# RWKV outputs of odd chunks with their two heads exchanged in PSUM

## The reference

```
def step(S, inp):
    r_t, w_t, k_t, v_t, kk_t, a_t = inp
    sa = jnp.einsum('bhvk,bhk->bhv', S, -kk_t)
    S = S * w_t[:, :, None, :] + sa[..., None] * (kk_t * a_t)[:, :, None, :] + v_t[..., None] * k_t[:, :, None, :]
    return S, jnp.einsum('bhvk,bhk->bhv', S, r_t)
...
y = _group_norm(y, ln_w, ln_b, RW_GN_EPS) + jnp.sum(r * k * r_k, -1, keepdims=True) * v
```

## Time and profile before

| what | us |
|---|---|
| median of 3 runs | 2271.08 (2270.03 to 2274.18) |
| profiled execution, its own time | 2267.93 |
| span in that execution | 2266.1 |
| PE busy | 2227.2 (98%) |
| POOL busy | 1742.7 (77%) |
| DVE busy | 1094.6 (48%) |
| ACT busy | 668.5 (30%) |

### The profile page before, as it was taken

One profiled execution on the slowest core, in us unless ns is written; L12 is line 12 of the kernel. 1 busy time (PEld: TensorE's weight loads), 2 busy tenths in 40 slices (PEclk: granted clock), 3 DMA queues, 4 the chain that ended last, 5 costly groups with the idle time before them and its releaser, 6 DMA issues. The chain is left out here.

```text
span 2266.1 us, 35428 instructions
## 1 busy us (share of the span) xinstructions
PE 2227.2 (98%) x14528; PEld 1715.4 (76%) x14528; DVE 1094.6 (48%) x1427; ACT 668.5 (30%) x1217; POOL 1742.7 (77%) x1228
## 2 busy tenths in 40 slices
PE   7999999999999999999999999999999999999999
PEld 5767777777778778777777677777777777777777
DVE  5023327566573762455260223386665647525542
ACT  5222322222221322443342222223233213324421
POOL 3677679688688999888637776896796799898884
PEclk9999999999999999999999999999999999999999
DMA  4623344333334545732436233443333354466223
GB/s 163 188 77 95 94 139 119 97 116 100 93 108 140 163 149 175 256 94 79 144 98 183 83 102 94 140 117 96 98 117 95 90 172 149 134 206 228 91 83 127
DMA packets 165475, 288.44 MB, mean 127 GB/s; under 512 B 28792, under 2 KB 36344, under 8 KB 163776
## 3 DMA queue, kind: packets, MB, share of 16 engines
q1 hardware_dynamic: 125216, 211.60, 31.4%
q10 hardware_dynamic: 40096, 74.57, 10.0%
HBM read 234.43 MB, written 51.68 MB: 126 GB/s over the span
## 5 line engine op out<-in xcount | busy, mean ns | idle before, releaser
L753 POOL TENSOR_SCALAR w_hi<-raw 128x512 fp32r<-128x512 f32 x552 | 902.3, 1635 | 322.5 <-PE ps_proj L794 275.9
L763 POOL TENSOR_TENSOR w_lo<-raw,w_hi 128x512 fp32r<-128x512 f32 (+1 forms) x640 | 846.0, 1322 | 153.7 <-ACT w_hi L1230 98.3
L794 PE MATMUL ps_proj<-h_hi,w_hi 128*128 128x512 f32 (+1 forms) x1760 | 725.2, 412 | 7.1 <-POOL w_lo L763 3.9
L794 PE MATMUL ps_proj<-h_lo,w_hi 128*128 128x512 f32 (+1 forms) x1760 | 688.9, 391 | 0.0
L794 PE MATMUL ps_proj<-h_hi,w_lo 128*128 128x512 f32 x1728 | 676.2, 391 | 0.0
L794 PEld LDWEIGHTS ps_proj<-h_hi,w_hi 128*128 128x128 f32 (+1 forms) x1760 | 330.2, 188 | 106.1 <-issue 27.3
L794 PEld LDWEIGHTS ps_proj<-h_lo,w_hi 128*128 128x128 f32 (+1 forms) x1760 | 329.6, 187 | 72.8
L794 PEld LDWEIGHTS ps_proj<-h_hi,w_lo 128*128 128x128 f32 x1728 | 326.1, 189 | 66.0 <-issue 7.7
L809 PE MATMUL ps_proj<-w_hi,h_hi 128*128 128x512 f32 x448 | 181.4, 405 | 0.4 <-POOL w_lo L763 0.4
L809 PE MATMUL ps_proj<-w_lo,h_hi 128*128 128x512 f32 x448 | 174.9, 390 | 0.0
L809 PE MATMUL ps_proj<-w_hi,h_lo 128*128 128x512 f32 x448 | 174.9, 390 | 0.0
(11 more groups left out here) (342 smaller groups left out, 2887.5 us busy)
## 6 DMA issues: line engine op xcount, KB each, us to landing
raw<-in_w_in_dram SPq DMA_DIRECT2D x480, 256.0 KB, 2.7
raw<-in_w_out_dram SPq DMA_DIRECT2D x128, 256.0 KB, 3.0
projected<-stage SPq DMA_DIRECT2D x116, 256.0 KB, 2.7
arena<-projected ACTq DMA_DIRECT2D x90, 256.0 KB, 3.1
out_dram<-arena ACTq DMA_DIRECT2D x7, 1024.0 KB, 4.8
gated_hi<-arena ACTq DMA_DIRECT2D x24, 256.0 KB, 2.6
gated_lo<-arena ACTq DMA_DIRECT2D x24, 256.0 KB, 3.2
h_hi<-gated_hi SPq DMA_DIRECT2D x8, 768.0 KB, 6.0
```

The lines of the kernel that those rows point to most:

```text
L753: nc.gpsimd.tensor_scalar(hi, src, 1.0, None, ALU.mult).then_inc(s_hi_split, 1)
L763: nc.gpsimd.tensor_tensor(lo, src, hi.bitcast(F32), ALU.subtract).then_inc(s_raw_split, 1)
L794: last = mm(ps_proj[rows, m, :], lhsT, rhs, start=(k == 0 and j == 0), stop=(k == KT - 1 and j == len(products) - 1))
```

## The change

The outputs of odd chunks are written with the two heads exchanged: head 0 to the upper partitions, head 1 to the lower. For the chunk's own outputs this changes the target partitions of the products alone. The carried products of odd chunks move from the diagonal quarters to the other two. ACT and DVE, which read these outputs, put the halves back: the one instruction over all chunks becomes three, one over even chunks with 128 partitions and two over odd chunks with 64 partitions each, reading one half and writing the other. In the table a tile moves from after line 1110 to before it, for every pair.

```
-    rw_carried=(3, 3, 3, 3), rw_gate=(13, 14, 13, 12),
+    rw_carried=(4, 4, 4, 4), rw_gate=(12, 13, 12, 11),
...
-                                mm(ps[half, 2 + c, fed], rw_vT[q, i, half], rw_gk[q, 4 * h + i, 64:P],
+                                mm(ps[halves[h ^ c], 2 + c, fed], rw_vT[q, i, half], rw_gk[q, 4 * h + i, 64:P],
                                    start=(i == 0), stop=False)
...
-                                mm(ps[half, 2 + c, fed], rw_pu[q, 4 * h + i, 64:P], rw_gb[q, 4 * h + i, 64:P],
+                                mm(ps[halves[h ^ c], 2 + c, fed], rw_pu[q, 4 * h + i, 64:P], rw_gb[q, 4 * h + i, 64:P],
                                    start=False, stop=False)
...
-                                last = mm(ps[half, 2 + c % 2, fed], rw_st[half, c, :],
+                                last = mm(ps[halves[h ^ (c % 2)], 2 + c % 2, fed], rw_st[half, c, :],
                                           rw_ar[half, c // 2, 1, 64 * (c % 2):64 * (c % 2) + 64],
...
-                        nc.scalar.activation(rw_kk.rearrange("p (i c t) -> p c i t", i=NT, c=2), y_parts, ACT.Square).then_inc(s_rw_y_squared, 1)
+                        squares = rw_kk.rearrange("p (i c t) -> p c i t", i=NT, c=2)
+                        nc.scalar.activation(squares[0:64, 1], y_parts[64:P, 1], ACT.Square)
+                        nc.scalar.activation(squares[64:P, 1], y_parts[0:64, 1], ACT.Square)
+                        nc.scalar.activation(squares[:, 0], y_parts[:, 0], ACT.Square).then_inc(s_rw_y_squared, 1)
...
-                        link(v.tensor_tensor(rw_yl.rearrange(in_parts, i=NT, c=2), rw_nr.rearrange(in_parts, i=NT, c=2), y_parts, MUL))
+                        scaled, scales = rw_yl.rearrange(in_parts, i=NT, c=2), rw_nr.rearrange(in_parts, i=NT, c=2)
+                        link(v.tensor_tensor(scaled[:, 0], scales[:, 0], y_parts[:, 0], MUL))
+                        link(v.tensor_tensor(scaled[0:64, 1], scales[0:64, 1], y_parts[64:P, 1], MUL))
+                        link(v.tensor_tensor(scaled[64:P, 1], scales[64:P, 1], y_parts[0:64, 1], MUL))
```

## The result

| what | before | after |
|---|---|---|
| median of 20 runs each, us | 2270.64 (2265.38 to 2274.18) | 2274.59 (2269.7 to 2277.23) |
| ratio, with its 95% interval | | 1.0014 (1.0008 to 1.0021) |
| profiled execution, us | 2267.93 | 2275.65 |

The ratio is +3.2 us at 2270.6 (1.8 to 4.8). The forecast was -0.8, and 2274.59 lies above the range, whose end was 2273.8. The prediction had put the smallest change that can be told from none at 0.2%; with 20 runs on each side the interval is narrower than that and lies wholly above 1. So this is a small loss, under the 0.2%, shown by many runs and by no single one.

A forecast was written before the change was run, and what follows sets the result against it. PE was taken as the bound, busy 2227.2 of 2266.1 us. Saving 2.8 us at line 1104 less 2.0 us of waits for DVE gave -0.8 us, 2270.3 us against the median 2271.08; range 2267.0 to 2273.8.

The forecast's parts named there:

- PE's part: Line 1104's carried products take 0.62 instead of 0.97 us, saving 0.35 a pair, 2.8 us over 8 pairs.
- Rival 2: Off-diagonal and diagonal passes don't overlap at line 1104: no gain, waits as forecast, +2.0, 2273.1 us; chance 0.10.
- ACT's part: One square becomes three, 0.54 us more at most, hidden before line 1110 even without the moved tile.
- DVE's part: Line 1942 in three parts takes 0.65 us more; with the moved tile DVE is 1.35 us late against PE.
- Crossing 1: From pair 1 to 2: DVE's chain falls into POOL's line 763, PE waits 0.7 us at line 979.
- Crossing 2: From pair 2 to 3: DVE 1.35 us later still ends before line 979 is due, no wait.
- Crossing 3: From pair 3 to 4: PE waits 0.3 us at line 979, between 0.1 and 0.7; none at line 986.
- The step that failed: Behind the fourth pair, before mLSTM's first product: a string of tiles, so no wait counted.
- The sum's range: Range of the total by the bounds of PE's waits, 0.2 to 3.7 us a layer: 2268.7 to 2272 us.
- Rival 1: DVE's lateness is absorbed, PE waits at most 0.4 us in all: -2.4 to -2.8, 2268.5 us; chance 0.27.
- Rival 3: DVE bounds every crossing, `s_y_ready` 2.7 us later, waits at line 979 3.6 a layer: +4.4, 2275.5 us; chance 0.13.
- the lock that the prediction weighed: DVE and POOL share ports exclusively, which lengthens DVE's delay; without it the net would be -2.4 us, not -0.8.

The follow-up runs named there:

- E1: Kernel before with only the exchange of the three products' targets on PE, halves not put back, old table: 2267.07 us, 0.9982.
- E2: The whole change with the old table of tiles, so no tile moved across line 1110: 2268.03 us, 0.9988 against the kernel before.
- E4: The change with mLSTM's copy three tiles earlier, three tiles going from ahead of line 1122 to ahead of line 1133: 2269.97 us, 0.9992 against before.
- E8: The change, new table, with mLSTM's copy one tile earlier: 2268.38 us, 0.9993 against the kernel before.
- E6: The whole change with the old table and mLSTM's copy three tiles earlier: 2268.09 us, 0.9988 against the kernel before.
- E10: Kernel before with the copy of line 1951, ahead of mLSTM's DVE chain, made three times: 2273.35 us, 1.0013.
- E3: Kernel before with the new table of tiles alone: 2271.78 us, 1.0005.
- E5: Kernel before with the three reads on ACT and DVE alone, no exchange, old table: 2272.55 us, 1.0007.
- E9: The change once more, word for word: 2271.8 us, 1.0010 against the kernel before.

## Why the prediction was wrong, step by step

- **PE's part: right.** 0.62 us was read from the earlier trace rows, 0.61 is there, in every kernel with the exchange; E1 has the gain by itself (-4.1, with 2.8 inside the interval). Rival 2 falls.
- **ACT's part: right.** The squares end 1.59 us before line 1110 with the moved tile, and in E2, without it, they are over at 435.36 and line 1110 starts at 436.26. The prediction had said that they would be in time without it, and that is why the tile is dispensable.
- **DVE's part: right.** The groups by shape of the kernel after, with the columns of the earlier trace rows:

```profile
L1946 DVE TENSOR_TENSOR arena<-arena,ps 128x256 f32<-128x256 f32 x8 | 3.4, 422 | 51.6 <-ACT arena L1271 51.6
...
L1947 DVE TENSOR_TENSOR arena<-arena,ps 64x256 f32<-64x256 f32 x8 | 3.4, 423 | 0.3
```

  424 ns was taken, 422 is there; half the partitions cost as much as all.
- **Crossing 1: right.** The gated output was put 12.7 us after the carried products, it comes at 12.73; a wait of 0.7 us was forecast, 0.69 is printed, 0.79 lost. **Crossing 2: right**, none. **Crossing 3: right in kind**, 0.14 where I took 0.3 between 0.1 and 0.7. Its second wait, at line 986, I had called "a long way off"; there were 1.99 us before, DVE came 2.4 us later, and PE lost 0.31 us in each layer. From the end of line 1678 to that of line 1845 it was 8.02 us in this crossing before, and it is 8.98 now (623.01 to 631.99). The sum at line 979 is 1.9 where 2.0 was forecast, and 0.6 at line 986 where nothing was.
- **The step that failed:** "Behind the fourth pair a string of tiles comes before mLSTM's first product, and I count no wait." The string of tiles is ahead of line 1122. Behind it a second chain of DVE ends at line 1133 with 0.3 us to spare, and that one was never looked at. It brings 3.3 us, and with it -0.8 would have been +2.5 (+3.1 with line 986), inside what was measured. E4 takes it away by covering the long form of the chain (-1.8), E8 with one tile and the short form (-1.6), E6 shows that the cover itself brings nothing, E10 makes it in the kernel before (+3.0).
- **The sum's range.** The prediction gave 2268.7 to 2272 "by the bounds of the waits". Its upper bound of 3.7 us a layer makes 2271.08 - 2.8 + 7.4 = 2275.7, so the end of 2272 does not follow from it, and the stated range, up to 2273.8, was narrower on the slow side than its own bounds.
- **Rival 1**, absorbed, falls by the waits at line 979. **Rival 3**, DVE as the bound at every crossing, falls too: the side that it foresaw came, at 2274.59 near its 2275.5, but the waits at line 979 are 0.93 a layer, under its 1.4, and there is none in crossing 2. That its number was near is luck: one more blocked operation did make the loss, but in mLSTM, where it did not look.

On the lock that the prediction weighed, the Trainium skill, SBUF — State Buffer, section "SBUF: two separate sides", says that a DVE operation with two SBUF inputs (against a GpSimd operation that reads SBUF) or in a two-port mode and a GpSimd operation take the shared ports as a lock: whichever starts first has them for the whole instruction, and the other is blocked. The rows of mLSTM agree in both directions for line 763: POOL takes 1.98 us when line 1979 got there first, and an operation of DVE on 128 elements takes 1.44 when POOL did. For line 753, POOL's operation with one input, the rows don't agree with "for the whole instruction": see the last section.

**What stays open.** Why line 971 in the second layer waits 0.8, 2.4 or 3.6 us from one execution to the next was not tried. E3 and E5 lie at +1.1 and +1.6 with intervals that hold zero and reach to 3.2 and 3.6; their rows show no new wait, so a cost of that size there is neither shown nor excluded. Inside the second pair of the first layer, from line 986 to line 1104, PE takes 65.9 us in the change and 65.6 in E9 but 65.2 and 64.7 in E4 and E8, which have the same RWKV (64.8 before); why was not tried either. And why POOL comes 0.24 us earlier against DVE's copy is read and not tested: in the kernel after, POOL starts the line 763 ahead of the copy 28.32 us after the fourth pair's carried products, before 28.54, it seems because DVE held it up for shorter in that pair's gate (its line 753 took 1.49, 1.67 and 1.93 us where it took 1.57, 1.93 and 1.94). E2 and E3 have 28.41 and 28.40, so each half of the change shifts it in part.

## What to carry to other kernels

When an engine that is off the path shares a lock with a steady stream of another, list every place where PE waits on it with little slack (here 0.3 us at line 1133, which turned into a loss of 1.6, and 2.0 at line 986, which turned into a loss of 0.3), not only those right behind the edit: a shift of a quarter of a microsecond upstream cost more than one operation of that stream (1.3 us) there. Test a cover before it is paid for: the three reads needed no more time than there was, and E2, which leaves the table alone, keeps the gain of 2.7 us that the moved tile turned into a loss. Moving a tile from ahead of such a release to behind it (one in E8, three in E4) took the wait away and, by E6, cost nothing that was seen. One tile was enough in E8 because the chain came in its short form; the long one, 14.4 to 15.0 us with the copies, would not have fitted in 13.97.

## What the runs showed of the hardware

- The length of one and the same chain of 13 operations of DVE beside POOL's stream goes with where its first operation starts behind the start of POOL's line 763, in steps and not in a slope. From that first start to the end of the last it is 13.3 us at 0.52 us (E8), 12.9 at 0.96 (before, E1), 12.8 at 1.09 to 1.10 (E2, E3, E5), 14.7 at 1.19 (the change, E9), 14.5 at 1.37 (E10) and 14.3 at 1.9 to 2.0 (E6, E4). A tenth of a microsecond, from 1.10 to 1.19, makes 1.87 us.
- Once the first operation is placed, the rest repeats: the twelve others have two forms only (12.25 and 13.7 us), operation by operation, in both layers. The close order far down the chain, POOL's line 763 at 738.90 and DVE's at 738.91, is part of the long form and came out the same way in both layers of the change, of E9 and of E10.
- POOL's two operations do not hold DVE up alike. In the trace of the kernel before, DVE's operations of 512 elements with two inputs in SBUF take 0.69 us with POOL idle. All 146 that start inside line 763 (two inputs), at least 0.15 us ahead of its end, end about 0.55 us behind it. Of the 237 that start so inside line 753 (one input) 141 end ahead of it, typically by 0.33 us, and their median is 0.98 us.
- An operation that reads PSUM on 64 partitions takes as long as on 128, on DVE (423 and 422 ns for 256 elements) and on ACT (0.38 and 0.39 us).
